# The first body of a hybrid trunk kernel: a second pair of ma projections on unnormed x, its tokens loaded in another order, and one seven-product unit fewer

## The reference, cut to what matters

```
h  = concat(meta, x)                                  # 528 x 2048
hn = rms_norm(h, norm_g)
xa, sa, vb, gb, sb, ma, mb = split(hn @ w_in, 7)      # w_in 2048 x 14336
ya = rg_lru(causal_conv4(xa), w_r, w_i, lambda) * silu(sa)
yb = causal_conv31(vb * sigmoid(gb))
yb = silu(layer_norm(yb)) * silu(sb)
merged = sigmoid(ma) * (ya @ w_proj_a) + sigmoid(mb) * (yb @ w_proj_b)
out = rms_norm(h + merged @ w_out, final_g)[meta dropped]
```

## Time and profile before

| what | us |
|---|---|
| median of three runs | 1765.79 |
| the profiled execution | 1768.35 |
| its span, first to last instruction | 1766.5 |
| TensorE busy in the span | 1742.7 |
| VectorE busy | 1313.7 |
| ScalarE busy | 867.7 |
| GpSimd busy | 298.0 |
| mean granted TensorE clock | 0.995 |

### The profile page before, as it was taken

One profiled execution on the slowest core, in us unless ns is written; L12 is line 12 of the kernel. 1 busy time (PEld: TensorE's weight loads), 2 busy tenths in 40 slices (PEclk: granted clock), 3 DMA queues, 4 the chain that ended last, 5 costly groups with the idle time before them and its releaser, 6 DMA issues.

```text
span 1766.5 us, 26382 instructions
## 1 busy us (share of the span) xinstructions
PE 1742.7 (99%) x10796; PEld 1574.0 (89%) x10796; DVE 1313.7 (74%) x1561; ACT 867.7 (49%) x1106; POOL 298.0 (17%) x331
## 2 busy tenths in 40 slices
PE   9899999999999999999999999999999999998998
PEld 8899999999999988888888888888888888887886
DVE  7969888888888888788878777898633297764431
ACT  6556555565565523555565555555422264433322
POOL 0502213112222100111211111222100111110000
PEclk9999999999999999999999999999999999999999
DMA  6247768567686665877765767785767679757422
GB/s 208 78 126 167 180 161 178 147 153 178 163 174 147 149 183 146 211 212 219 208 171 160 199 167 211 189 216 177 231 223 232 183 201 203 164 149 262 150 83 95
DMA packets 285656, 311.55 MB, mean 176 GB/s; under 512 B 9440, under 2 KB 239968, under 8 KB 284384
## 3 DMA queue, kind: packets, MB, share of 16 engines
q1 hardware_dynamic: 211024, 188.21, 33.9%
q0 software_dynamic: 74512, 121.65, 31.7%
HBM read 235.38 MB, written 45.09 MB: 159 GB/s over the span
## 4 chain that ended last, share of the span: by engine, by line
PE 93%; DVE 3%; issue 2%; DMA 1%; ACT 1%; POOL 0%; SPq 0%; DVEq 0%; POOLq 0%; ACTq 0%
PE psum L889 28%; PE psum L798 25%; PE psum L759 17%; PE psum L802 13%; PE psum L981 7%; PE psum L995 3%; PE psum L856 1%; DMA t_parts<-m_spill 1%; DVE t_parts L1823 0%; DVE region L1914 0%; DMA region<-in_x_channels 0%; DVE region L1537 0%; DVE x_parts L1698 0%; DVE w_lo L1691 0%; DVE total L1579 0%
## 5 line engine op out<-in xcount | busy, mean ns | idle before, releaser
L1225 ACT ACTIVATE w_hi<-raw 128x1024 fp32r<-128x1024 f32 x110 | 116.3, 1057 | 283.8 <-PE psum L759 137.0
L1471 DVE SCALAR_TENSOR_TENSOR region<-region,params 128x512 f32<-128x512 f32 x368 | 250.6, 746 | 0.0
L1691 DVE TENSOR_TENSOR w_lo<-raw,w_hi 128x1024 fp32r<-128x1024 f32 x110 | 134.9, 1227 | 127.5 <-ACT w_hi L1225 127.5
L889 PE MATMUL psum<-x_parts,w_hi 128*128 128x264 f32 x1792 | 227.1, 284 | 0.0
L889 PEld LDWEIGHTS psum<-x_parts,w_hi 128*128 128x128 f32 x1792 | 222.0, 188 | 0.0
L1698 DVE TENSOR_TENSOR w_lo<-region,w_hi 128x1024 fp32r<-128x1024 f32 x108 | 131.9, 1223 | 70.4 <-ACT w_hi L1241 70.2
L1698 DVE TENSOR_TENSOR x_parts<-region,x_parts 128x1024 fp32r<-128x1024 f32 x108 | 131.7, 1223 | 57.9 <-ACT x_parts L1241 57.9
L889 PE MATMUL psum<-x_parts,t_parts 128*128 128x264 f32 x1344 | 167.9, 284 | 0.0
L889 PEld LDWEIGHTS psum<-x_parts,t_parts 128*128 128x128 f32 x1344 | 165.2, 188 | 0.0
L798 PE MATMUL psum<-t_parts,x_parts 128*128 128x512 f32 x576 | 144.7, 393 | 1.4 <-ACT aux L1285 1.4
L798 PE MATMUL psum<-t_parts,w_hi 128*128 128x512 f32 x576 | 144.9, 393 | 0.2 <-ACT aux L1279 0.2
(11 more groups left out here) (221 smaller groups left out, 3106.4 us busy)
## 6 DMA issues: line engine op xcount, KB each, us to landing
raw<-in_w_in SPq DMA_DIRECT2D x112, 512.0 KB, 4.1
region<-in_w_in SPq DMA_DIRECT2D x56, 1024.0 KB, 6.3
wide<-region POOLq DMA_DIRECT2D x98, 256.0 KB, 5.0
region<-in_w_proj_b SPq DMA_DIRECT2D x16, 1024.0 KB, 8.5
raw<-in_w_out SPq DMA_DIRECT2D x32, 512.0 KB, 4.0
raw<-in_w_proj_a SPq DMA_DIRECT2D x31, 512.0 KB, 4.3
region<-in_w_in POOLq DMA_DIRECT2D x28, 512.0 KB, 7.6
sigmoid_spill<-wide POOLq DMA_DIRECT2D x16, 512.0 KB, 3.3
```

What stands on the lines that cost most here:

```text
L889: last = pe.matmul(psum[:, bank + h, 0:HALF], weights[:, k // 2, (k % 2) * P:(k % 2 + 1) * P], part[:, KH * half + k, h * HALF:(h + 1) * H ...
L1225: act.activation(cut_at(n)[0], raw_at(n).rearrange("p (k n) -> p k n", k=4), ACT.Copy).then_inc(hi_ready, 1)
L1471: ins = dve.scalar_tensor_tensor(conv_b[:, t, :], moved, w, conv_b[:, t, :], ALU.mult, ALU.add)
L1691: dve.tensor_tensor(lo, raw_at(n).rearrange("p (k n) -> p k n", k=4), hi.bitcast(F32), ALU.subtract).then_inc(lo_ready, 1)
```

## The change

The first body gets a second pair of ma, chunks 8 to 11, and its order becomes ma pair 0, xa, ma pair 1, gb, vb: 20 chunks. ma pair 0 comes first and needs no meta tokens. The plain pairs after the branches are then ma 2 to 4 instead of 1 to 3, and 27 units follow instead of 28. On SyncE's queue x tile 0 comes first, then the parameters, the first weights, x tile 1, x tiles 2 and 3, and then the meta tokens; the steps on the meta tokens move behind the first tiles on each engine. VectorE makes 4 lo parts of normed x, GpSimd 12.

```
-BODY, ITEMS_BODY = 16, 12
+BODY, ITEMS_BODY = 20, 12
-        LO_BY_DVE = 3
-        STD = 4
+        LO_BY_DVE = 4
+        STD = 5
         NX = 4 * PAIRS - STD
         C0 = BODY + (PAIRS - 1) * ITEMS_BODY
-        W0 = C0 + 4 * (STD - 1)
+        W0 = C0 + 4 * (STD - 2)
         A0 = W0 + 7 * NX
...
 # SyncE
-            sp.dma_start(meta_x, meta_channels).then_inc(meta_loaded, 16)
+            sp.dma_start(channels[:, 0, :], x_channels[:, 0, :]).then_inc(x_loaded[0], 16)
             sp.dma_start(params[:, :, :], parameters).then_inc(params_loaded, 16)
-            body(0, [c for col in (COL_XA, COL_MA, COL_GB, COL_VB) for c in columns(w_in_v, col)], x_too=True)
+            body(0, [c for col in (COL_MA, COL_XA, COL_MA + 256, COL_GB, COL_VB) for c in columns(w_in_v, col)], x_too=True)
 # in body(), behind the first weights
+                        sp.dma_start(channels[:, 1, :], x_channels[:, 1, :]).then_inc(second_loaded, 16)
                         sp.dma_start(channels[:, 2:4, :], x_channels[:, 2:4, :]).then_inc(x_loaded[1], 16)
+                        sp.dma_start(meta_x, meta_channels).then_inc(meta_loaded, 16)
...
 # TensorE
+                for g in range(4):
+                    multiply(0, g, x_tokens((6, 7)), g, raw_x=True)
+                    if g == 0:
+                        pe.wait_ge(meta_summed, 1)
+                        pe.matmul(psum[:, 4, 0:META], average[:, :], stats[:, 0:META], start=True, stop=True)\
+                            .then_inc(meta_mean, 1)
                 pe.wait_ge(meta_lo, 1)
                 for g in range(4):
-                    multiply(0, g, all_tokens(((0, 1), (2, 3))), g, raw_x=True)
+                    multiply(0, 4 + g, all_tokens(((0, 1), (2, 3))), g, mean=g == 0)
+                pe.wait_ge(ma_scaled, 2)
                 for g in range(4):
-                    multiply(0, 4 + g, x_tokens((4, 5)), g, mean=g == 0)
+                    multiply(0, 8 + g, x_tokens((4, 5)), g)
...
+                pe.wait_ge(first_ma_gated, 2)
                 for g in range(4):
                     gate_round(0, g)
...
-                    multiply(0, 8 + g, all_tokens(((0, 1), (2, 3))), g)
-                pe.wait_ge(first_ma_gated, 2)
+                    multiply(0, 12 + g, all_tokens(((0, 1), (2, 3))), g)
+                pe.wait_ge(second_ma_gated, 2)
...
 # ScalarE, first_body
-                raw_tiles(range(0, 2))
+                raw_tiles(range(0, 1))
+                cut_hi(0, 0)
+                raw_tiles(range(1, 4))
+                act.wait_ge(meta_loaded, 16)
+                act.activation(meta_squares, meta_x, ACT.Square).then_inc(meta_squared, 1)
+                raw_tiles(range(4, 8))
+                square_tiles(range(0, 4))
+                cut_hi(0, 1)
+                act.wait_ge(meta_mean, 1)
+                act.activation(psum[:, 4, 0:META], psum[:, 4, 0:META], ACT.Sqrt, bias=eps).then_inc(meta_rms, 1)
+                raw_tiles(range(8, 12))
+                square_tiles(range(4, 8))
                 act.wait_ge(meta_normed, 1)
                 act.activation(x_hi[:, :, 0:META], meta_x, ACT.Copy).then_inc(meta_hi, 1)
-                cut_hi(0, 0)
...
                 cut_hi(0, 2)
...
+                norm_tiles_hi(3)
                 cut_c_hi(0, 1)
+                act.wait_ge(first_ma_spilled, 16)
+                for t in range(2):
+                    act.wait_ge(ma_scaled, t + 3)
+                    act.activation(first_ma[:, t, :], psum[:, 4 + t, :], ACT.Sigmoid).then_inc(second_ma_gated, 1)
+                cut_hi(0, 14)
                 act.wait_ge(norm_lo_pool, 7 - LO_BY_DVE)
                 read_gates(0, 0)
...
 # VectorE, first_body
                     for j in range(4 * p, 4 * p + 4):
+                        if j == 1:
+                            cut_lo(0, 0)
...
+                    if p == 0:
+                        sum_meta()
+                    elif p == 1:
+                        norm_meta()
+                    elif p == 2:
+                        cut_meta_lo()
                 cut_lo(0, 4)
                 add_squares_of(range(12, CT))
                 cut_lo(0, 5)
                 dve.wait_ge(x_rms, 1)
-                one_step(dve.reciprocal(total[:, :], psum[:, 7, :]))
+                one_step(dve.reciprocal(total[:, :], psum[:, 5, :]))
+                scale_ma(4, 6)
                 cut_lo(0, 6)
-                norm_tiles(5)
-                norm_tiles(6)
+                norm_tiles(range(0, 8))
+                cut_lo(0, 7)
+                norm_tiles(range(8, CT))
+                cut_gates_lo(0)
+                cut_lo(0, 8)
+                cut_lo(0, 9)
+                cut_lo(0, 10)
+                for j in range(LO_BY_DVE):
+                    tile_lo(j)
                 unscaled_xa()
-                cut_lo(0, 7)
+                cut_lo(0, 11)
+                conv_a_taps(0, range(KA), (0,), conv)
+                cut_c_lo(0, 0)
+                cut_lo(0, 12)
                 dve.wait_ge(norm_lo_pool, 1)
-                conv_a_taps(0, range(KA), (0,), conv)
+                conv_a_taps(0, range(KA), (1,), conv)
+                cut_lo(0, 13)
+                scale_ma(12, 4)
                 cut_c_lo(0, 1)
...
```

More of the change, by code:

```diff
@@ L237, in hybrid_trunk @@
         gates_multiplied, gates_read = sem("gates_multiplied"), sem("gates_read")
-        first_ma_gated, first_ma_spilled, decay_ready, root_ready = (
-            sem("first_ma_gated"), sem("first_ma_spilled"), sem("decay_ready"), sem("root_ready"))
+        first_ma_gated, first_ma_spilled, second_ma_gated, second_ma_spilled = (
+            sem(f"{n}_ma_{what}") for n in ("first", "second") for what in ("gated", "spilled"))
+        decay_ready, root_ready = sem("decay_ready"), sem("root_ready")
         h_ready, h_spilled, h_loaded = sem("h_ready"), sem("h_spilled"), sem("h_loaded")
@@ L398, in spills @@
         def spills(w):
-            return sum(32 if n // PAIRS == SB else 16 for n in range(w % 2, w, 2) if n)
-        PLAIN_BANKS = {1: 6, 2: 0, 3: 3}
+            return sum(32 if n // PAIRS == SB else 16 for n in range(w % 2, w, 2) if n > 1)
+        PLAIN_BANKS = {2: 6, 3: 3, 4: 0}
         PA_BANKS = (0, 6, 2, 4)
@@ L413, in hybrid_trunk @@
         m_spill = nc.dram_tensor("m_spill", (CT, P, SEQ), F32, kind="Internal").ap()
-        OUT_STREAM = [divmod(n - n // 4, 8) if n % 4 < 3 else (LAST, n // 4) for n in range(2 * BODY)]
+        OUT_STREAM = [divmod(n - n // 4, 8) if n % 4 < 3 else (LAST, n // 4) for n in range(8 * (LAST + 1))]
         assert LAST == 3
@@ L425, in body @@
                 for p, source in enumerate(sources):
-                    if x_too and p < 4:
-                        for n in (2 * p, 2 * p + 1) if p else (0,):
+                    if x_too and 0 < p < 4:
+                        for n in (2 * p, 2 * p + 1):
                             sp.dma_start(channels[:, 2 * n:2 * n + 2, :], x_channels[:, 2 * n:2 * n + 2, :])\
@@ L652, in load_sigmoid @@
                 w = kind * PAIRS + i
-                pool.wait_ge(o_spilled[w % 2], spills(w + 2))
+                wait(pool, o_spilled[w % 2], spills(w + 2))
                 load_ln(spill[kind], i)
@@ L769, in multiply @@
                     pe.wait_ge(x_summed, CT - 1)
-                    pe.matmul(psum[:, 7, :], average[:, :], total[:, :], start=True, stop=True).then_inc(x_mean, 1)
+                    pe.matmul(psum[:, 5, :], average[:, :], total[:, :], start=True, stop=True).then_inc(x_mean, 1)
                 pe.wait_ge(lo_ready, plus(n, 1))
@@ L1090, in first_body @@
                 cut_c_hi(0, 2)
-                norm_tiles_hi(9)
-                cut_hi(0, 10)
+                cut_hi(0, 15)
                 read_gates(0, 1)
[L1094 to L1097, removed]
                 cut_c_hi(0, 3)
-                cut_hi(0, 11)
+                cut_hi(0, 16)
                 read_gates(0, 2)
@@ L1207, in branch_end @@
             def branch_end(i):
[L1209 to L1219, removed]
+                read_gates(0, 3)
+                cut_hi(i, 17)
+                v = decay_of(0)
+                cut_hi(i, 18)
+                root_of(v)
+                group_done(0, 16)
+                for t in range(2):
+                    gb_sigmoid_of(t, 2 * t)
+                cut_hi(i, 19)
             def chunk_hi(n):
@@ L1909, in tile_lo, with norm_tiles, scale_ma @@
                                   ALU.subtract).then_inc(norm_lo, 1)
-            def norm_tiles(p):
-                for j in NORM_TILES[p]:
+            def norm_tiles(tiles):
+                for j in tiles:
                     dve.scalar_tensor_tensor(channels[:, j, :], channels[:, j, :], params[:, j, NORM_G:NORM_G + 1],
                                              total[:, :], ALU.mult, ALU.mult).then_inc(x_normed, 1)
-                    if 1 <= j <= LO_BY_DVE:
-                        tile_lo(j - 1)
+            def scale_ma(chunks, bank):
+                group_done(0, chunks)
```

(5 more changed lines are left out.)

136 lines of the change are left out of this document (61 added, 75 removed).

## The result

| | median us | runs | ratio to before | 95% interval |
|---|---|---|---|---|
| before | 1765.79 | 7 | | |
| changed | 1773.74 | 7 | 1.004 | 1.003 to 1.005 |

The change makes the kernel slower by 0.4%. I had forecast 1764.9 with a range of 1760.0 to 1769.5, so both the direction and the range were wrong.

The account below looks back on a forecast made before the run. TensorE, busy 1742.7 of 1766.5 us, was taken as the bound. First body 17.5 later, a unit 19.55 less: -2.05; plus 1.2 for the ya cut: -0.85, so 1765.79 becomes 1764.9 us, range 1760.0 to 1769.5.

Parts of the forecast that it names:

- The rest of the first body: From chunk 4 to pair 1: gb starts at 82.3, no wait at the second gate round, end at 132.8, 17.5 us later.
- my second rival: Second gate round: its gate chain comes late, 3.3 us of wait plus 1.6 of clock, change costs +4.05 (1769.8); chance 14%.
- The wait of 3.3 us: TensorE's wait in the kernel before, read as the second gate round waiting for c_lo.
- the 1.3 us in two pieces: TensorE's waits in the kernel before's first 200 us, read as for cuts that ScalarE began late.
- The gaps that I took as gone: Gb and vb part: 6.2 us of gaps and half clock (3.3 + 1.3 + 1.6), all to vanish behind the extra ma pair.
- the term of 50.5: Time of the gb and vb part without gaps, 50.5 us, added to its start at 82.3 to give 132.8.
- The level of the kernel before: The difference of -0.85 us, found on the profiled execution (1768.35), was applied to the median 1765.79.
- The first 43 us: Start: TensorE begins at 9.1, 1.5 us earlier, but ScalarE and VectorE pace it; chunk 4 through at 42.6 against 42.02.
- The matmul work: TensorE: second ma pair adds 22.1 us, one unit fewer saves 19.55, so the work grows by 2.55 us.
- The ya chunk: End of the units: ScalarE's cut for the first ya chunk must await the last product; TensorE waits 1.2 us.
- The rival of falls in chunks 2 to 4: Start: the clock falls again, 1.6 us for one half-rate stretch, 4.8 for three; +0.75 to +3.95 us in all; chance 8%.
- a clock of 0.50 anywhere after 20 us: A listed sign that the forecast is wrong: granted clock at half rate anywhere after 20 us.

Follow-up runs that it names:

- gate_order: Changed kernel with the first round's gates read and chunk 14 cut before ma pair 1's sigmoids, and c_lo 1 cut earlier on VectorE: 1767.64 us.
- pool_wait: Changed kernel with GpSimd's subtractions for tiles 8 to 15 held back until VectorE has done the short convolution: 1766.72 us.
- before_gate: Kernel before with its third gate round's inputs made earlier (c_lo 2 before the norm of tiles 8 to 11, second round's gates behind c_hi 2): 1766.65 us.
- best: Changed kernel with the start of the kernel before, GpSimd held back for tiles 8 to 15, and a free place for the first ya chunk: 1761.78 us.
- before_again: The kernel before, unchanged, timed and profiled again: 1766.98 us.
- old_start: Changed kernel with the start of the kernel before (meta tokens first, xa as chunks 0 to 3, then both ma pairs): 1769.99 us.
- both: Changed kernel with the gates read and c_lo cut earlier, and the first ya chunk cut into a free place: 1767.21 us.
- ya_place: Changed kernel with the first ya chunk cut into a free place instead of the last product's: 1770.97 us.
- after_again: The changed kernel, unchanged, timed and profiled again: 1772.58 us.

## Why the prediction was wrong, step by step

- **The rest of the first body: the step that failed.** I wrote that of the gb and vb part "I take all of it as gone" and that the second gate round "just fits", with the gates read at 88.8. They were read at 92.4. The wait for them was to be 0 and was 3.8 us, and the clock's fall behind it cost 1.6 more: 5.4 us, over the 4.9 that I had given as its upper bound. The size that was off is VectorE beside GpSimd. I priced a tap there at 1.1 us from the earlier trace rows, where 3.29 us for three is a mean over mixed company: in the kernel before GpSimd stopped at 65.44, 1.1 us after those taps began. Beside GpSimd all the time three took 5.13, 1.7 each, and the cut behind them 2.3 instead of 1.15. That made VectorE's scaling end at 90.1 instead of 86.2, and c_lo, at 1.5 us, came behind it. The mechanism was my second rival, to which I gave 14%: 3.3 + 1.6 forecast for it, 3.8 + 1.6 measured. gate_order and pool_wait take it away in two ways. A chain with 0.1 us of room on an estimate of 17 us should have had even odds.
- **Two readings of the kernel before.** The wait of 3.3 us was that of the third gate round, not the second. And the 1.3 us in two pieces were not for cuts that ScalarE began late: TensorE began these chunks at 76.34 and 85.92, just when GpSimd's lo parts ended (76.24 and 85.82), and the kernel has it wait for them there, though the view names no releaser ("issue"). These are waits of the norm chain: in before_gate, where c_lo and the gates come earlier, the first of them is named and has grown to 4.76 us. TensorE's rounds and GpSimd in the kernel before:

```profile
58.61 0.28 PE L856 MATMUL psum<-c_hi,gate_hi 128*128 128x264 f32 x1
...
65.19 0.29 PE L856 MATMUL psum<-c_hi,gate_hi 128*128 128x264 f32 x1
...
75.20 0.36 PE L856 MATMUL psum<-c_hi,gate_hi 128*128 128x264 f32 x1 [3.26 <-DVE c_lo L1552]
```

```profile
59.67 5.77 POOL L670 TENSOR_TENSOR x_parts<-region,x_parts 128x512 fp32r<-128x512 f32 x3 [6.32 <-ACT x_parts L1043]
70.16 6.08 POOL L670 TENSOR_TENSOR x_parts<-region,x_parts 128x512 fp32r<-128x512 f32 x4 [4.72 <-ACT x_parts L1043]
78.73 7.09 POOL L670 TENSOR_TENSOR x_parts<-region,x_parts 128x512 fp32r<-128x512 f32 x4 [2.49 <-ACT x_parts L1043]
```

- **The gaps that I took as gone.** They were there to be had. The gb and vb part takes 56.7 or 56.8 us from the first gate round to the first item of pair 1 in all three profiles of before, and 49.8 us in pool_wait and in best, where nothing waits. So the term of 50.5 was 0.7 too large; in the changed kernel it took 55.3.
- **The level of the kernel before.** I carried a difference between profiles over to the median, as if both profiles were equally unlucky. The one of before was 2.6 us above its median, that of the changed kernel 1.9 below its own. Only a little of that lies at the start: chunk 4 was through at 42.02 there, at 41.67 in before_again and 41.29 in before_gate. The falls of the clock behind the 4.5 us wait in the output projection differ too: the chunk there took 6.43 us in before, 5.42 in before_gate and 5.97 in after.
- **The first 43 us.** Right in each step but the fall of the clock in chunk 0, which changed nothing (chunk 1 at 17.3, measured 16.68; chunk 3 at 29.8, 29.09; chunk 4 through at 42.6, 42.28): ScalarE and VectorE pace it, and starting TensorE earlier buys nothing. Against 40.52 in old_start, and with 1.0 us less matmul work done by then, the new start loses 2.8 us. In the sum it is 1.6 (42.6 - 42.02 and that 1.0). Against the three profiles of before it measured 1.3 to 2.0. Why these begin later than the three with the same start and the second pair (chunk 4 through at 40.52, 40.89 and 40.32; first weights cut from 8.0 to 8.5, not from 8.9 to 9.2) stays open: the order of the loads and steps up to there is the same.
- **The matmul work.** Right: the pair costs 22.1 (59.88 to 82.01 in after). From pair 1 to the first ya chunk before takes 1126.92 us and both, without the ya wait, 1107.37: a unit gives back 19.55.
- **The ya chunk.** Right: 1.30 us for 1.2.
- **The clock.** The rival of falls in chunks 2 to 4 did not come about in the profile after; the waits of 1.45, 0.72, 1.20 and 0.65 us left it at full. In ya_place's profile it fell at 16 to 21, behind a wait of 1.73 us, with a chunk of 7.36 us. The Trainium skill (TensorE: Matmul & The Clock Gate, section "A second HAM failure mode: psum-queue depth-cycling") says that frequent very short idling can make the clock swing. One fall at the start in the six profiles with the new start neither shows nor excludes that. As a sign of being wrong, "a clock of 0.50 anywhere after 20 us" could decide nothing: both kernels have it near 1600 us, behind the wait of 4.5 us.

From profile to profile: the first body ends 137.35 - 115.30 = 22.05 later, less 19.55, plus 1.30 is 3.8, and the spans differ by 1770.1 - 1766.5 = 3.6. I had -0.85, so the miss is 4.4 us, and the failed step accounts for it: 5.4, less the 0.7 by which the gap-free part was too large and 0.3 won at the start. From median to median the change costs 8.0 us, and 6.1 with after_again. What is above 3.6 is the place of the two profiles among their executions. The two medians of the changed kernel, 1773.74 and 1772.58, differ by 1.2 us; that the fall behind the gate wait can be 1.1 us longer is shown by after_again, that it makes this difference is not.

## What to carry to other kernels

Work put in front of a chain covers only the part of it that does not depend on that work: here the new sigmoids and scalings were queued ahead of the very gates that TensorE needed next. When a whole forecast rests on a chain that just fits, price its operations in the company that they will have, not by a mean over mixed company. And ask a profile how typical it is before its gaps are booked as gain: compare its time with the median, and its half-clock stretches with the mean clock of the other runs.

## What the runs showed of the hardware

- While GpSimd subtracted without pause, VectorE's operations on SBUF took longer. Three taps took 5.13 us beside it (1.7 each, where one subtraction of GpSimd took 1.66) and 2.38 without, a weight cut 2.31 and 1.22, and the first tap, which reads one tensor and a factor per channel, 1.53 and 0.55 (after and pool_wait); c_lo took 1.52 and 0.42 (gate_order, the second at 93.53 behind GpSimd's end). It is not so for every one: a c_lo of pool_wait took 0.43 at 85.45 with GpSimd at work. The two scalings of a product in PSUM took 1.28 us beside GpSimd (after) and 1.30 without (old_start, at 57.56). GpSimd's eight subtractions took 13.28 us in after and 13.37 in pool_wait, where they were held back: they only moved.
- Behind long waits the clock fell every time; how long it stayed down differs. In the twelve profiles a stretch at 0.50 began in or just behind every wait of TensorE of 3.2 to 4.8 us: the wait among the gate rounds in seven of them, the one in the output projection in all twelve, and the one of 3.7 us in before_again's units. Behind the same gate wait of 3.8 us it lasted 3.4 us in after and about 7 in after_again. At the start it fell behind the wait of 2.88 us in before and that of 1.73 in ya_place, but not behind 1.72 in before_again, 1.85 in both, 2.06 in before_gate, nor behind any of those of 1.20 to 1.50 us.
